# Moving the last residual tile's x ahead of its square and of the next weights' low part, in a two-block fp32 kernel

## The reference, cut to what matters

```
first_block:  h = h + gla_mixer(rmsnorm(h));  h = h + swiglu(rmsnorm(h))
              h = h + dsa_mixer(rmsnorm(h));  h = h + swiglu(rmsnorm(h));  rmsnorm(h)
second_block: h = h + recurrent_block(rmsnorm(h));  h = h + sqrelu_mlp(rmsnorm(h))
              k, v = shared_kv(rmsnorm(h));  q = rmsnorm(h) @ w_q
              h = h + band_attention(q, k, v) @ w_o;  h = h + sqrelu_mlp(rmsnorm(h))
rmsnorm(x, g) = x * rsqrt(mean(x*x, axis=-1) + eps) * g
```

## Time and profile before

| | |
|---|---|
| median of 3 runs | 1181.04 us (1179.45 to 1181.84) |
| the profiled execution's own time | 1181.85 us |
| its span, first to last instruction | 1180.0 us |
| busy: TensorE (PE) / weight load (PEld) | 1166.8 us (99%) / 1137.8 us (96%) |
| busy: VectorE (DVE) / ScalarE (ACT) / GpSimd (POOL) | 820.7 us (70%) / 693.8 us (59%) / 89.3 us (8%) |
| mean granted TensorE clock | 0.999 |

### The profile page before, as it was taken

How to read it: one execution, slowest core, us unless ns; L and a number is a source line. 1 busy time by engine, 2 the same in 40 slices (tenths; PEclk the granted TensorE clock), 3 DMA queues, 4 the chain that set the end, 5 groups by cost and what they waited for, 6 DMA issues and landing times. The chain is left out here.

```text
span 1180.0 us, 25998 instructions
## 1 busy us (share of the span) xinstructions
PE 1166.8 (99%) x9738; PEld 1137.8 (96%) x9738; DVE 820.7 (70%) x1301; ACT 693.8 (59%) x1120; POOL 89.3 (8%) x97
## 2 busy tenths in 40 slices
PE   9999999999999999999999999999999999999998
PEld 8999999999998899999999989999999979999998
DVE  7767866666578877666668997675567677777543
ACT  6635765654455667665556976664447576666432
POOL 1000200000110020000120000000013223000000
PEclk9999999999999999999999999999999999999999
DMA  7532555556664336666664555566666424566663
GB/s 275 174 94 89 194 178 178 178 178 189 203 203 144 107 110 192 192 192 191 211 213 152 189 179 191 190 199 188 205 213 206 141 79 152 185 194 195 202 194 107
DMA packets 57578, 207.85 MB, mean 176 GB/s; under 512 B 6352, under 2 KB 7568, under 8 KB 57248
## 3 DMA queue, kind: packets, MB, share of 16 engines
q1 hardware_dynamic: 57136, 203.52, 54.8%
q0 software_dynamic: 288, 3.21, 0.7%
q10 hardware_dynamic: 80, 0.07, 0.0%
HBM read 205.66 MB, written 1.05 MB: 175 GB/s over the span
## 5 line engine op out<-in xcount | busy, mean ns | idle before, releaser
L1702 DVE TENSOR_TENSOR w_lo<-w_raw,w_hi 128x1024 fp32r<-128x1024 f32 x379 | 463.2, 1225 | 68.0 <-ACT w_hi L514 67.1
L514 ACT CAST w_hi<-w_raw 128x1024 fp32r<-128x1024 f32 x379 | 395.1, 1045 | 172.6 <-PE acc L1012 170.8
L1010 PE MATMUL acc<-x_hi,w_hi 128*128 128x256 f32 (+1 forms) x1688 | 478.0, 283 | 1.6 <-DVE w_lo L1702 0.8
L1011 PE MATMUL acc<-x_lo,w_hi 128*128 128x256 f32 (+1 forms) x1688 | 473.1, 280 | 0.0
L1012 PE MATMUL acc<-x_hi,w_lo 128*128 128x256 f32 (+1 forms) x1688 | 472.7, 280 | 0.0
L1010 PEld LDWEIGHTS acc<-x_hi,w_hi 128*128 128x128 f32 x1688 | 317.6, 188 | 5.7 <-DVE x_lo L1722 1.8
L1011 PEld LDWEIGHTS acc<-x_lo,w_hi 128*128 128x128 f32 x1688 | 317.8, 188 | 0.5
L1012 PEld LDWEIGHTS acc<-x_hi,w_lo 128*128 128x128 f32 x1688 | 317.7, 188 | 0.0
L1010 PE MATMUL acc<-m_hi,w_hi 128*128 128x256 f32 x512 | 141.3, 276 | 0.0
L1011 PE MATMUL acc<-m_lo,w_hi 128*128 128x256 f32 x512 | 141.3, 276 | 0.0
L1012 PE MATMUL acc<-m_hi,w_lo 128*128 128x256 f32 x512 | 141.3, 276 | 0.0
(11 more groups left out here) (372 smaller groups left out, 1673.6 us busy)
## 6 DMA issues: line engine op xcount, KB each, us to landing
w_raw<-weights SPq DMA_DIRECT2D x381, 512.0 KB, 4.2
bias<-bias_rows POOLq DMA_DIRECT2D x1, 2048.0 KB, 9.3
h<-hT SPq DMA_DIRECT2D x4, 272.0 KB, 5.0
bias<-bias_rows POOLq DMA_DIRECT2D x1, 1088.0 KB, 8.7
outT<-h SPq DMA_DIRECT2D x4, 256.0 KB, 4.6
con<-constants SPq DMA_DIRECT2D x1, 913.0 KB, 9.0
w_raw<-weights SPq DMA_DIRECT2D x2, 256.0 KB, 3.8
par<-cols SPq DMA_DIRECT2D x1, 84.0 KB, 2.3
```

Of the source, the lines that this page charges most:

```text
L514: nc.scalar.copy(w_hi[:, slot, :], w_raw[:, slot, :]).then_inc(hi_ready, 1)
L1010: nc.tensor.matmul(out, wh, xh[:, k, tok], start=first and n == 0, stop=False)
L1011: nc.tensor.matmul(out, wh, xl[:, k, tok], start=False, stop=False)
L1702: V.tensor_tensor(w_lo[:, slot, :], w_raw[:, slot, :], w_hi[:, slot, :].bitcast(F32), ALU.subtract)\
```

## The change

At the seams, for the last tile (n = 7): ACT makes `x_hi` ahead of the square, and the in-line copy `xl_hi` only behind the tile loop; DVE makes `x_lo` ahead of the `w_lo` of the coming unit, and `xl_lo` behind the loop. At the lru_out seam ACT makes both x of the last pair and then both squares, and DVE adds the squares of tiles 5, 6 and 7 behind the last `x_lo`. In `relu_mlp` the cast of unit FIRST+4 stands ahead of the wait for the eviction of the first unit. No operation is added or removed.

```diff
@@ -523,9 +523,10 @@
 
             def make_x(gain, n, tok, hi=x_hi):
                 nc.scalar.activation(hi[:, n, tok], h[:, n, tok], ACT.Copy, scale=col(gain, n)).then_inc(xhi_ready, 1)
-                if hi is xs_hi and n == KD - 1:
-                    nc.scalar.activation(xl_hi[:, n, tok], h[:, n, tok], ACT.Copy, scale=col(gain, n))\
-                        .then_inc(xhi_ready, 1)
+
+            def make_last_in_line(gain, tok):
+                n = KD - 1
+                nc.scalar.activation(xl_hi[:, n, tok], h[:, n, tok], ACT.Copy, scale=col(gain, n)).then_inc(xhi_ready, 1)
 
             def square(n, tok, dyn=False):
                 nn = bass.ds(n, 1) if dyn else slice(n, n + 1)
@@ -542,13 +543,17 @@
                     for k in range(kunits):
                         ahead(phase, kunits * n + k)
                     act.wait_ge(acc_free, tile_read(phase, n))
+                    if gain and n == KD - 1:
+                        make_x(gain, n, tok, hi)
                     square(n, tok)
-                    if gain:
+                    if gain and n < KD - 1:
                         make_x(gain, n, tok, hi)
                     if gain == "final_a":
                         act.wait_ge(s_("gain_root"), 1)
                         nc.scalar.activation(sqg[:, n, tok], h[:, n, tok], ACT.Square, scale=final_s[:, n:n + 1])\
                             .then_inc(s_("sqg_ready"), 1)
+                if hi is xs_hi:
+                    make_last_in_line(gain, tok)
 
             allt, xt = slice(0, T), slice(META, T)
             def split_next(*units):
@@ -871,7 +876,11 @@
                 for n in (2 * pair, 2 * pair + 1):
                     act.wait_ge(acc_free, tile_read("lru_out", n))
                     make_x("mlp_norm0", n, xt, xs_hi)
-                    square(n, xt)
+                    if pair < 3:
+                        square(n, xt)
+            square(6, xt)
+            square(7, xt)
+            make_last_in_line("mlp_norm0", xt)
 
             def relu_mlp(layer, norm):
                 base = FF2T * layer
@@ -884,11 +893,13 @@
 
                 def step(i, j):
 
-                    ahead(ph, j, 4, i)
+                    if j != 1 or not isinstance(i, int):
+                        ahead(ph, j, 4, i)
                     if j or not isinstance(i, int):
                         lead(4 * i + (j - 1), j - 1)
                     else:
                         root(norm, xt)
+                        ahead(ph, 1, 4, i)
                     act.wait_ge(acc_free, tile_read(ph, 4 * i + j))
                     nc.scalar.activation(y2_s[:, j % 2, :], y_s[:, j % 2, :], ACT.Square).then_inc(s_("y2_ready"), 1)
 
@@ -1722,11 +1733,13 @@
                 V.scalar_tensor_tensor(out=lo[:, n, tok], in0=h[:, n, tok], scalar=col(gain, n),
                                        in1=hi[:, n, tok].bitcast(F32), op0=ALU.mult, op1=ALU.subtract)\
                     .then_inc(x_ready, 1)
-                if hi is xs_hi and n == KD - 1:
-                    dve.wait_ge(xhi_ready, first + KD + 1)
-                    V.scalar_tensor_tensor(out=xl_lo[:, n, tok], in0=h[:, n, tok], scalar=col(gain, n),
-                                           in1=xl_hi[:, n, tok].bitcast(F32), op0=ALU.mult, op1=ALU.subtract)\
-                        .then_inc(x_ready, 1)
+
+            def make_last_in_line(gain, tok, first):
+                n = KD - 1
+                dve.wait_ge(xhi_ready, first + KD + 1)
+                V.scalar_tensor_tensor(out=xl_lo[:, n, tok], in0=h[:, n, tok], scalar=col(gain, n),
+                                       in1=xl_hi[:, n, tok].bitcast(F32), op0=ALU.mult, op1=ALU.subtract)\
+                    .then_inc(x_ready, 1)
 
             def inverse(norm, tok):
                 dve.wait_ge(std_ready, NORM[norm] + 1)
@@ -1740,9 +1753,13 @@
                         ahead(phase, kunits * n + k)
                     unit_done(phase, kunits * n + kunits - 1)
                     V.tensor_tensor(h[:, n, tok], h[:, n, tok], acc[n % 4][:, 0:n_tok], ALU.add).then_inc(acc_free, 1)
+                    if gain and n == KD - 1:
+                        make_x_lo(gain, n, tok, XB[norm], hi, lo)
                     ahead(phase, kunits * n + kunits - 1)
-                    if gain:
+                    if gain and n < KD - 1:
                         make_x_lo(gain, n, tok, XB[norm], hi, lo)
+                if hi is xs_hi:
+                    make_last_in_line(gain, tok, XB[norm])
 
             allt, xt = slice(0, T), slice(META, T)
             V.memset(eps[:, 0:1], EPS).then_inc(setup, 1)
@@ -2110,8 +2127,12 @@
                 unit_done("dsa_out", max(m, 1))
                 src = acc[0][:, m * SEQ:(m + 1) * SEQ] if m < 2 else acc[m % 4][:, 0:SEQ]
                 V.tensor_tensor(h[:, m, xt], h[:, m, xt], src, ALU.add).then_inc(acc_free, 1)
+                if m == KD - 1:
+                    make_x_lo("norm_ffn1", m, xt, XB["ffn1"], xs_hi, xs_lo)
                 ahead("dsa_out", m)
-                make_x_lo("norm_ffn1", m, xt, XB["ffn1"], xs_hi, xs_lo)
+                if m < KD - 1:
+                    make_x_lo("norm_ffn1", m, xt, XB["ffn1"], xs_hi, xs_lo)
+            make_last_in_line("norm_ffn1", xt, XB["ffn1"])
             gated_mlp(1, xt)
 
 
@@ -2311,11 +2332,13 @@
                 if pair < 3:
                     split_lru(26 + pair)
                 for n in range(max(2 * pair - 2, 1), 2 * pair):
-                    add_output_square(n)
+                    if n < 5:
+                        add_output_square(n)
                 for n in (2 * pair, 2 * pair + 1):
                     make_x_lo("mlp_norm0", n, xt, XB["mlp0"], xs_hi, xs_lo)
-            add_output_square(6)
-            add_output_square(7)
+            for n in (5, 6, 7):
+                add_output_square(n)
+            make_last_in_line("mlp_norm0", xt, XB["mlp0"])
 
             def relu_mlp(layer, norm):
                 base = FF2T * layer
@@ -2437,8 +2460,12 @@
                 unit_done("o2", max(m, 1))
                 src = acc[0][:, m * SEQ:(m + 1) * SEQ] if m < 2 else acc[m % 4][:, 0:SEQ]
                 V.tensor_tensor(h[:, m, xt], h[:, m, xt], src, ALU.add).then_inc(acc_free, 1)
+                if m == KD - 1:
+                    make_x_lo("mlp_norm1", m, xt, XB["mlp1"], xs_hi, xs_lo)
                 ahead("o2", m)
-                make_x_lo("mlp_norm1", m, xt, XB["mlp1"], xs_hi, xs_lo)
+                if m < KD - 1:
+                    make_x_lo("mlp_norm1", m, xt, XB["mlp1"], xs_hi, xs_lo)
+            make_last_in_line("mlp_norm1", xt, XB["mlp1"])
             relu_mlp(1, "mlp1")
             for n in range(KD):
                 for k in range(4):
```

## The result

The changed kernel takes 1183.51 us (median of 20 runs, 1182.22 to 1185.5), the kernel before 1181.3 us on the same chip (20 runs, 1179.18 to 1184.23). The ratio is 1.0018 with a 95% interval of 1.0012 to 1.0025: slower by 1.4 to 3.0 us, an interval that has 0.2% (2.36 us) inside it. The profiled execution has a span of 1182.4 us, against 1180.0, and its own time is 1185.5 us.

The account below looks back on a forecast made before the run. TensorE is busy 1166.8 of 1180.0 us, so only its own waits, some 13 us, can be won. 2.05 + 1.06 - 0.80 = +2.31 on 1181.04 gives about 1183.3 us; 8 in 10 from 1179.1 to 1184.6.

Parts of the forecast that it names:

- A `w_lo` that starts first holds POOL to its end: At the POOL seams: POOL's add starts 0.15 us behind `w_lo` and ends 0.60 behind its end, at 444.99 instead of 443.94.
- Rival 1: At the POOL seams: `w_lo` does not hold POOL, five seams win at most 2.10; total -2.90 us, 1178.1; chance 0.12.
- Five seams at +0.41: gla_out, ffn0_out, dsa_out, mlp0_out and o2 each get 0.41 us longer because the sum of squares waits for POOL; +2.05 together.
- The 0.31: At each of the five seams: the sum of squares starts later, 445.05 instead of 444.74 at dsa_out, +0.31 us.
- The 0.10 behind it: At each of the five seams: a sum that was waited for takes 0.70 us instead of 0.60, +0.10.
- lru_in at +1.06: At ffn1_out to lru_in: POOL's second add ends behind `xl_lo`, TensorE starts its sum at 626.69 instead of 625.63, +1.06 us.
- Rival 3: In the recurrent block: the shift at lru_in is absorbed, +1.06 falls away; total +1.25 us, 1182.3; chance 0.12.
- lru_out at -0.38 and -0.42: At lru_out to mlp0_in: sum of squares 0.38 us sooner, gap before unit FIRST+4 gone for 0.42; -0.80 together.
- Rival 4: At lru_out: the seam wins nothing because the chain there finds another link; total +3.1 us, 1184.1; chance 0.10.
- The sum: Whole kernel: the five seams, lru_in and lru_out terms, 2.05 + 1.06 - 0.80, give +2.31 us.
- Rival 2: At the POOL seams: POOL starts first and `w_lo` waits; five seams -2.10, lru_in +1.04, total -1.86 us, 1179.2; chance 0.10.

Follow-up runs that it names:

- add_first: The changed kernel plus a DVE wait for POOL's add of the last square between `x_lo` and `w_lo`; 1179.03 us against 1180.99, ratio 0.998.
- lru_only: The changed kernel with only the lru_out edit and the earlier `relu_mlp` cast kept, residuals in old order; 1180.6 us against 1180.99, ratio 0.9994.
- act_part: The changed kernel, but DVE makes `w_lo` ahead of `x_lo` again; 1179.89 us against 1180.99 for the kernel before, ratio 0.9988.
- dve_part: The changed kernel, but ACT squares the last tile ahead of its `x_hi` again; 1178.89 us against 1180.99 for the kernel before, ratio 0.9978.
- half_w_lo: The changed kernel, with the `w_lo` behind the last `x_lo` made in two halves; 1180.63 us against 1181.5 for the kernel before, ratio 0.9994.
- cast_only: The kernel before with only the cast of unit FIRST+4 moved ahead of the eviction wait in `relu_mlp`; one execution, 1183.91 us.
- mix: The changed kernel with DVE waiting for POOL's last add at five seams, ACT squaring ahead of `x_hi` at lru_in; 1177.5 us against 1181.5, ratio 0.9964.

## Why the prediction was right, point by point

- **A `w_lo` that starts first holds POOL to its end.** Shown. The predicted distance was 0.15 us between the two starts and 0.60 between the two ends; measured 0.13 and 0.58 at dsa_out, 0.13 and 0.59 at lru_in. The Trainium skill, "SBUF — State Buffer", section "Who interferes with whom", says that a VectorE instruction with two SBUF inputs contends with a GpSimd instruction that reads SBUF, and that the order of issue decides who blocks; the trace agrees, with the 1.67 at 444.06 where `w_lo` starts first and the 0.74 of add_first where POOL does. Rival 1 is out.
- **Five seams at +0.41.** The 0.31 is right: 0.30 at all five. The 0.10 behind it is mis-sized at three. Between the sum and the next landmark TensorE loses 0.10 to 0.11 more at gla_out and ffn0_out, but 0.19 to 0.20 at dsa_out, mlp0_out and o2, so the five cost 2.30 us instead of 2.05. In TensorE's timeline of the changed kernel the matmuls of two units behind the sum at dsa_out start every 0.118 us, in the kernel before those of one unit, and all later ones every 0.113. Why a unit behind a wait is slower was not tested. In the second execution of the kernel before, the first unit runs at 0.114 already, 0.09 less in all, so part of this goes with the execution; it stays open.
- **lru_in at +1.06.** Measured +1.03, by the chain that was predicted: `xl_lo` ahead of the second add. What happened in the recurrent block is not settled: TensorE makes up 0.26 us there (0.08 and 0.18), but two executions of the kernel before differ by 0.18 and 0.15 in the same places. Rival 3, the whole shift absorbed, is out: 0.77 of it is left.
- **lru_out at -0.38 and -0.42.** The first is -0.36. The second came to -0.30: at the gap itself TensorE gains 0.41, but in the changed kernel and in lru_only it loses 0.1 in the units between the sum and the gap; act_part, dve_part, add_first, half_w_lo and cast_only have no such loss and show -0.40 or -0.41. The second execution of the kernel before loses 0.16 in the same units and has it back at the gap, where it waits for `w_lo` anyway; with the gap gone, such a loss counts. The term is right for the gap; why the units sometimes take longer has no cause that I can show. Rival 4 is out.
- **The sum.** 2.30 + 1.03 - 0.26 - 0.66 = 2.41 by the timelines, against 2.31; the spans differ by 2.4 us and the medians by 2.2. The mechanism and the order of each seam came out as predicted; that the total is right to 0.1 us is luck, for the errors were +0.25 at the five seams, -0.29 at and behind lru_in and +0.14 at lru_out, and they cancel.
- **Rival 2, POOL wins the race,** did not happen in the changed kernel; add_first makes it happen. The five seams then win 1.78 us where the rival had 2.10: the full 0.42 at those of 256 columns, but only 0.28 and 0.22 at gla_out and ffn0_out, where the prediction had carried over the wait of dsa_out.

## What to carry to other kernels

When two engines hold each other up, a reordering has to be costed by who starts first, to a tenth of a microsecond: here each of two good moves gained, and together they let a 1.2 us subtraction start 0.13 us ahead of a 0.74 us add on which TensorE waited. Before an operand is hurried along, ask what its engine will do in the time that comes free, and whether that is long and can wait; a wait that holds back such an instruction until the short urgent one is through cost DVE 0.8 us of idling and gained TensorE 0.7 us at a 256-column seam (1.19 to 0.46). Where the effect is 0.2% of the run, distances between the same two instructions at the seam tell more than the spans.

## What the hardware showed unexpectedly

TensorE's granted clock can fall in the middle of a long busy run, in some executions of a program and not in others. The view of windows of TensorE, columns: stretch; its length, busy us (instructions), granted clock, DMA share, GB/s. First the kernel before:

```profile
66.00:68.00 2.00, 1.76 (x10) 1.00 0.62 135
68.00:70.00 2.00, 2.00 (x14) 0.66 0.31 127
70.00:72.00 2.00, 2.00 (x10) 0.50 0.00 0
72.00:80.00 8.00, 8.00 (x70) 1.00 0.21 66
```

And the same program in its second execution, before_again:

```profile
66.00:68.00 2.00, 1.77 (x11) 1.00 0.50 160
68.00:70.00 2.00, 2.00 (x19) 1.00 0.25 102
70.00:72.00 2.00, 2.00 (x19) 1.00 0.00 0
72.00:80.00 8.00, 8.00 (x72) 1.00 0.20 66
```

In both TensorE has just had a short wait (1.76 and 1.77 busy of 2.00 us) and then works without a gap; in the first it gets the lower of its two levels, 1.2 GHz (0.50), by 70 us and 2.4 GHz again in the stretch from 72 us. This is the -1.58 us between the two executions before 110 us. The profiles of before, after, act_part and cast_only have it (cast_only once more, at 11 to 14 us), the other six do not; as before and before_again are one program, it goes with the execution and not with the edit. What decides it is open. It goes with much of the spread of single runs: of the 17 of the kernel before beside mix, the nine with a mean granted clock of 1.000 have a median of 1180.1 us, the four at 0.999 one of 1181.95. That is as large as most effects studied here. The spans of before and after, 1180.0 and 1182.4, both have one such stretch in them, so their difference is not its doing.

The second thing is the turn-taking in half_w_lo and, in the changed kernel, at lru_in: the engine that was kept waiting goes ahead of the next instruction of the one that held it, so two long queues alternate instruction by instruction, and each instruction seems longer by what it waited (1.74 for a `w_lo` of 1.22, 1.16 for an add of 0.74).
